# Modulation of layer 0 as 32-bit matmuls of unsplit weights on four column tiles of the array

## The reference, cut to what matters

```python
def ada_params(cond, w, b):
    mod = jax.nn.silu(cond) @ w + b          # w: 2048 x 6144
    return jnp.split(mod, 3, axis=-1)        # shift, scale, gate

sh_l, sc_l, g_l = ada_params(c, ada_w[0], ada_b[0])
sh_c, sc_c, g_c = ada_params(c_ctx, ada_w[0], ada_b[0])
xm_l = x_lat * (1.0 + sc_l) + sh_l
xm_c = x_ctx * (1.0 + sc_c) + sh_c
...
mem_n = rmsnorm(mem, norm_mem_w)             # mem: 256 x 2048
k = mem_n @ w_k                              # 2048 x 2048
```

## Time and profile before

| | us |
|---|---|
| median of 3 runs | 3157.62 |
| the runs | 3156.45, 3160.35, 3157.62 |
| span of the profiled execution | 3157.5 |
| PE busy, share of the span | 98% |
| DVE busy, ACT busy | 70%, 52% |
| first "w" unit starts on PE | 24.88 |
| last "a" unit ends on PE, "w" unit 22 starts | 165.45 |

### The profile page before, as it was taken

How to read it: one execution, slowest core, us unless ns; L and a number is a source line. 1 busy time by engine, 2 the same in 40 slices (tenths; PEclk the granted TensorE clock), 3 DMA queues, 4 the chain that set the end, 5 groups by cost and what they waited for, 6 DMA issues and landing times.

```text
span 3157.5 us, 45097 instructions
## 1 busy us (share of the span) xinstructions
PE 3086.2 (98%) x16842; PEld 2654.5 (84%) x16842; DVE 2218.5 (70%) x2768; ACT 1640.1 (52%) x2000; POOL 53.6 (2%) x52
## 2 busy tenths in 40 slices
PE   7999999999999999999999999999999999999998
PEld 6788878888788887888888888888888888888887
DVE  7779877788677777656757855567456777777544
ACT  6665444546534566544556655445345555555443
POOL 0011300000000000000000000000000000000000
PEclk9999999999999999999999999999999999999999
DMA  8978675787568765655555565566345555555554
GB/s 297 351 249 287 239 276 201 282 323 237 176 221 282 254 203 181 206 173 189 172 188 172 168 199 187 189 226 197 135 150 184 187 186 186 187 191 194 189 190 139
DMA packets 180248, 666.42 MB, mean 211 GB/s; under 512 B 20084, under 2 KB 20468, under 8 KB 178808
## 3 DMA queue, kind: packets, MB, share of 16 engines
q1 hardware_dynamic: 178424, 660.09, 61.7%
q10 hardware_dynamic: 1664, 4.19, 0.3%
HBM read 657.91 MB, written 6.29 MB: 210 GB/s over the span
## 4 chain that ended last, share of the span: by engine, by line
PE 85%; DVE 7%; DMA 4%; ACT 2%; DVEq 1%; issue 1%; ACTq 0%; SPq 0%
PE acc L762 45%; PE acc L766 22%; PE acc L773 4%; PE acc L775 4%; PE acc L774 4%; DVE w_lo L1990 3%; DMA ada_raw<-in_w_ada 2%; ACT w_hi L1277 1%; DMA mod_raw<-in_w_mod 1%; DVE mod_raw L2001 1%; PE acc L930 1%; DMA raw<-in_w_mix_out 0%; PE msc L1172 0%; PE msc L876 0%; PE msc L1192 0%
## 5 line engine op out<-in xcount | busy, mean ns | idle before, releaser
L1990 DVE TENSOR_TENSOR w_lo<-raw,w_hi 128x1024 fp32r<-128x1024 f32 x1020 | 1242.3, 1227 | 564.1 <-ACT w_hi L1277 554.6
L1277 ACT CAST w_hi<-raw 128x1024 fp32r<-128x1024 f32 x1020 | 1061.8, 1049 | 805.6 <-PE acc L766 571.3
L762 PE MATMUL acc<-a_pair,w_hi 128*128 128x512 f32 x2944 | 931.6, 398 | 4.6 <-DVE a_pair L2905 2.4
L766 PEld LDWEIGHTS acc<-a_pair,w_lo 128*128 128x128 f32 x2944 | 554.1, 188 | 131.1
L766 PE MATMUL acc<-a_pair,w_lo 128*128 128x256 f32 x2944 | 579.3, 278 | 0.0
L762 PE MATMUL acc<-b_pair,w_hi 128*128 128x512 f32 x1792 | 569.4, 399 | 5.3 <-DVE w_lo L1990 5.2
L762 PEld LDWEIGHTS acc<-a_pair,w_hi 128*128 128x128 f32 x2944 | 451.2, 189 | 7.6 <-DVE a_pair L2905 2.8
L762 PE MATMUL acc<-f_pair,w_hi 128*128 128x512 f32 x1408 | 442.4, 395 | 0.0
L766 PEld LDWEIGHTS acc<-b_pair,w_lo 128*128 128x128 f32 x1792 | 337.5, 188 | 79.8
L766 PE MATMUL acc<-b_pair,w_lo 128*128 128x256 f32 x1792 | 353.0, 278 | 0.0
L766 PEld LDWEIGHTS acc<-f_pair,w_lo 128*128 128x128 f32 x1408 | 264.5, 188 | 62.5
(11 more groups left out here) (364 smaller groups left out, 2749.5 us busy)
## 6 DMA issues: line engine op xcount, KB each, us to landing
raw<-in_w_ffn_up SPq DMA_DIRECT2D x176, 512.0 KB, 3.9
mod_raw<-in_w_mod SPq DMA_DIRECT2D x128, 512.0 KB, 5.2
raw<-in_w_ffn_down SPq DMA_DIRECT2D x88, 512.0 KB, 3.3
ada_raw<-in_w_ada SPq DMA_DIRECT2D x64, 512.0 KB, 5.5
raw<-in_w_xa_k SPq DMA_DIRECT2D x32, 512.0 KB, 6.1
raw<-in_w_k SPq DMA_DIRECT2D x32, 512.0 KB, 4.6
raw<-in_w_v SPq DMA_DIRECT2D x32, 512.0 KB, 4.8
raw<-in_w_even_out SPq DMA_DIRECT2D x32, 512.0 KB, 4.6
```

The costliest lines, as they stand in the source:

```text
L762: pe.matmul(acc[:, bank(stage, g) + m, :], w_h[:, cols], pair[:, :, kc, :], start=begin, stop=False, skip_group_check=True)
L766: mm = pe.matmul(acc[:, bank(stage, g) + m, 0:T], w_l[:, cols], pair[:, 0, kc, :], start=False, stop=end, skip_group_check=True)
L1277: nc.scalar.copy(w_hi[:, slot], source).then_inc(hi_done, 1)
L1990: vec.tensor_tensor(w_lo[:, slot], source, w_hi[:, slot].bitcast(F32), ALU.subtract).then_inc(lo_done, 1)
```

## The change

The "a" units leave the walk of `mem_k`, which has 32 places now instead of 96. They keep the four buffers `ada_raw`, but these are now a ring of their own: PE reads them directly as 32-bit operands, without rounding and subtraction by ACT and DVE, and frees them itself (`ada_used`). Two units (a pair, four chunks of 128 rows) are taken by four matmuls of 32 stationary columns each (`cond_tile`, two of them filled), one for each quarter of the output partitions: the four chunks' partial sums land on partitions 0 to 31, 32 to 63, 64 to 95 and 96 to 127 of the same PSUM bank. Four pairs make a group of 512 columns. ACT copies all 128 partitions of a group to `mod_rows`; PE multiplies each 128 x 128 block of it with `mod_pick`, a matrix of zeros and ones with two columns, which turns the rows into columns and adds the four partial rows.

```diff
-ADA_FIRST = 6
+ADA_TILES = 4
...
-    Stage("mem_k", "w_xa_k", "F", 1, groups=4, ada=(0, ADA_UNITS), dve=1),
+    Stage("mem_k", "w_xa_k", "F", 1, groups=4, dve=1),
...
+ADA_PAIRS = ADA_UNITS // 2
+ADA_AT = {j: range(j * ADA_PAIRS // ADA_OVER, (j + 1) * ADA_PAIRS // ADA_OVER) for j in range(ADA_OVER)}
+GROUP_PAIRS = DC // ADA_TILES
+ADA_LAST = {g: next(j for j in ADA_AT if GROUP_PAIRS * (g + 1) - 1 in ADA_AT[j]) for g in range(ADA_GROUPS)}
...
-CTX_LOAD_AT = 84
-MEM_SQUARE_AT = {2: 0, 5: 1, 8: 2, 11: 3}
-MEM_SUM_AT = {7: 0, 10: 1, 13: 2, 15: 3}
-MEM_ROOT_AT, MEM_SCALE_AT, MEM_TURN_AT, MEM_TAKE_AT = 16, 17, 22, 27
+CTX_LOAD_AT = 21
+MEM_SUM_AT = 2
+MEM_ROOT_AT, MEM_SCALE_AT, MEM_TURN_AT, MEM_TAKE_AT = 3, 3, 6, 8
+
+MOD_ROWS_AT = {}
+for _g, _j in ADA_LAST.items():
+    MOD_ROWS_AT.setdefault(max(_j, 1), []).append(_g)
+MOD_SUM_AT = {}
+for _j, _gs in MOD_ROWS_AT.items():
+    MOD_SUM_AT.setdefault(min(max(_j + 2, MEM_TAKE_AT + 1), CTX_AT - 2), []).extend(_gs)
...
             def load_first(stage):
 
+                load_mem()
                 for j, (kind, g, k, _) in enumerate(stage.kinds):
...
+                    if j >= RING:
+
+                        sp.wait_ge(lo_done, j + 1)
+                    nc.sync.dma_start(raw[:, j % RING].rearrange("p a b -> p (a b)"),
+                                      t[stage.weights][stage.group_units * g + k]).then_inc(raw_landed[j % RING], 16)
+                    if j == 0:
+                        load_constants()
+                    for pair in ADA_AT.get(j, ()):
+                        for n in (2 * pair, 2 * pair + 1):
+                            if n >= ADA_RING:
+
+                                sp.wait_ge(ada_used, (n - ADA_RING) // 2 + 1)
+                            nc.sync.dma_start(ada_raw[:, n % ADA_RING].rearrange("p a b -> p (a b)"),
+                                              t["w_ada"][n]).then_inc(ada_landed[n % ADA_RING], 16)
...
+            def modulation(pair):
+
+                g, quarter = divmod(pair, GROUP_PAIRS)
+                if quarter == 0:
+
+                    pe.wait_ge(ada_free, g + 1)
+                if pair == 0:
+                    pe.wait_ge(act_step, AFTER["cond"]["act"])
+                for n in (2 * pair, 2 * pair + 1):
+                    pe.wait_ge(ada_landed[n % ADA_RING], 16 * (n // ADA_RING + 1))
+                for tile in range(ADA_TILES):
+                    n, c = 2 * pair + tile // KU, tile % KU
+                    rows = slice(tile * (P // ADA_TILES), (tile + 1) * (P // ADA_TILES))
+                    mm = pe.matmul(msc[rows, 1 + g % 3, :], cond_tile[:, ADA_TILES * quarter + tile, :],
+                                   ada_raw[:, n % ADA_RING, c, :], start=(quarter == 0), stop=(quarter == GROUP_PAIRS - 1))
+                mm.then_inc(ada_used, 1)
+
             def mem_sums(j):
...
+                for pair in ADA_AT.get(j, ()):
+                    modulation(pair)
+                if j == MEM_SUM_AT:
+                    pe.wait_ge(consts_in, 48)
+                    for q in range(4):
...
+                for g in MOD_SUM_AT.get(j, ()):
+
+                    pe.wait_ge(ada_free, 3 + g + 1)
+                    if g == 0:
+
+                        pe.wait_ge(dve_step, AFTER["mem_norm"]["dve"])
+                    for c in range(4 * g, 4 * g + 4):
+                        mm = pe.matmul(msc[:, 0, T + 2 * c:T + 2 * c + 2], mod_rows[:, c * P:(c + 1) * P], mod_pick,
+                                       start=True, stop=True)
...
+                for g in MOD_ROWS_AT.get(j, ()):
+
+                    act.wait_ge(ada_used, GROUP_PAIRS * (g + 1))
+                    nc.scalar.copy(mod_rows[:, g * NCOL:(g + 1) * NCOL], msc[:, 1 + g % 3, :]).then_inc(ada_free, 1)
```

More of the change, by code:

```diff
@@ L99, in __init__ @@
             groups, group_units = 2 * groups, group_units // 2
-        self.group_units, self.groups, self.ada, self.gate = group_units, groups, ada, gate
+        self.group_units, self.groups, self.gate = group_units, groups, gate
         self.n_w = groups * group_units
         self.kinds = [("w", *divmod(n, group_units), (n + 1) % group_units == 0) for n in range(self.n_w)]
[L104 to L112, removed]
         if gate:
@@ L189, in ring_place @@
 def ring_place(stage, j):
[L191 removed]
+    return stage.u0 + j
 def spread(n, k):
@@ L219 @@
 STATES_AT = 9
-assert all(kind[0] == "w" for kind in STAGE["mem_k"].kinds[MOD_TURN - 1:])
+assert max(MOD_ROWS_AT) < MOD_TURN
 KV_GROUP = {"mem_k": 0, "mem_va": 4, "mem_vb": 5}
@@ L469, in build @@
         mod_raw = sb("mod_raw", [P, MOD_RING, KU * NCOL])
-        mod_rows = place("mod_rows", [4, 32 * P], F32, cond_wide_at)
+        mod_rows = place("mod_rows", [P, 32 * P], F32, cond_wide_at)
         assert at[0] - cond_wide_at >= 32 * P * 4
@@ L710, in run @@
                             side(j)
-                        if kind == "a":
-                            ada_bank = 1 + g % 3
-                            if first:
-                                pe.wait_ge(ada_free, g + 1)
-                            pe.wait_ge(lo_done, i * stage.n + (u + 1 + RING))
-                            for c in range(KU):
-                                kc = KU * k + c
-                                pe.matmul(msc[:, ada_bank, :], cond_pair[:, kc, :], w_hi[:, slot, c, :],
-                                          start=(first and c == 0), stop=False)
-                                mm = pe.matmul(msc[:, ada_bank, :], cond_pair[:, kc, :], w_lo[:, slot, c, :],
-                                               start=False, stop=(last and c == KU - 1))
-                            mm.then_inc(unit_used, 1)
-                            continue
                         if kind == "x":
@@ L823, in mem_sums @@
                     steps.end("mem_norm")
[L824 to L829 removed]
+                for g in MOD_SUM_AT.get(j, ()):
[5 more added lines that the diff above has]
+                                       start=True, stop=True)
+                    if g == ADA_GROUPS - 1:
+                        steps.done(mm)
+                        steps.end("mod")
             run("mem_k", b_pair, 0, batch=2, side=mem_sums)
```

133 lines of the change are left out of this document (47 added, 86 removed).

## The result

The changed kernel takes 3182.26 us, the median of four runs (3176.46 to 3187.03), against 3158.98 for the kernel before in the same session (3156.45 to 3161.31): ratio 1.0074, 95% interval 1.0063 to 1.0086. It is slower by 23 us. Four runs more in another session gave 1.0073 (1.0052 to 1.0094). The profiled execution of the changed kernel is the slowest of its four, with a span of 3185.2 us, 27.7 above the span before.

The account below looks back on a forecast made before the run. PE, with DMA and DVE near their limits: start and work 160.5, waits 9, 3.6 and 4.4, clock 5.5 put "w" unit 22 at 183.0 against 165.45; less 1.3 back, 3157.5 + 16.3 = 3173.8 us, range 3155 to 3216.

Parts of the forecast that it names:

- the start of "w" unit 22: First stage, PE, after the last modulation units: any shift moves the program's end equally; forecast 183.0 us against 165.45 before.
- the alternation: PE switching tiling mode between "w" units and pairs, 44 times: 0.3 us a place taken, 6.6 us up to unit 22.
- The step on the pairs: Four 32-bit matmuls per pair on PE: only neighbouring tiles' records overlap, 2.15 us alone, 1.72 where another follows, 64.5 in all.
- the first rival: Pairs on PE: four column tiles run wholly in parallel, 0.86 us a pair, transfers set the time; 3160 us, chance 0.26.
- the half overlap: Pairs on PE: a tile's second record overlaps the next tile's first, 2.15 us a pair alone; the forecast, 3166 to 3184, chance 0.42.
- The rival of tiles wholly beside each other: Pairs on PE at 0.86 us each; transfers bound the stage, two-pair ring runs dry; 3160 us, range 3154 to 3168, chance 0.26.
- the wait at place 9: First 0/1 matmuls: PE idle about 9 us for DVE's scale copy, behind unit 11's subtraction, its transfer queued behind pair 15.
- The other waits: PE waiting for ACT's copies to `mod_rows` at places 12 to 21, 3.6 us, and for the context, 4.4 us.
- The clock term: PE's lower clock after idleness at the start, place 9 and the context: three times 1.6 to 2.1, 5.5 us.
- Tiles one after the other: Pairs on PE: the four column tiles don't overlap, 3.45 us a pair; 3214 us, chance 0.20.
- The queue stays fed: Transfers of the first stage: tiles wholly parallel and dry times mostly covered; 3143 us, floor 3135, chance 0.12.
- After unit 22: PE's 32 transposes (2.11 us) become one group of eight records (0.86): 1.3 us back, and no slack to absorb the delay.

## Why the prediction was right, and where it was not

Forecast were 3173.8 us, range 3155 to 3216, with 0.68 for slower. The time was 3182.3, slower by 0.74%. Sign and range hold, and the size is off by 8.5 us. The moment that the prediction summed, the start of "w" unit 22, was forecast at 183.0 and came at 191.4. That looks like a small miss of one term, and is the sum of large misses with opposite signs:

| term, us | forecast | in the trace |
|---|---|---|
| first pair starts | 15 | 15.1 |
| 22 "w" units and the alternation | 61.2 + 6.6 | 66.0 (22 x 3.0) |
| pairs | 64.5 | 32 (32 x 1.0) |
| squares, transposes of the scale | 7.2 | 7.2 |
| seven groups of 0/1 matmuls | 6.0 | 6.4 (0.92 each) |
| PE's waits | 17.0 | 39.8 |
| lower clock | 5.5 | 24.9 |
| "w" unit 22 | 183.0 | 191.4 |

The middle rows give the work at the higher clock; the last term is what units (15.6), groups (4.8) and pairs (4.5) took beyond it.

- **The step on the pairs failed.** It said that a tile's two records follow each other and records start in order, so that tiles half overlap and a pair costs 2.15 us alone. It costs 1.00. The Trainium skill ("TensorEngine Tiling (Array Packing)", Key Properties) says that different tiles can load and multiply in parallel. The trace agrees, with 1.00 us against 3.55 us on one tile. I had its result as the first rival, and should have given it the larger chance; the half overlap rested on a guess about the order of starts that no row showed.
- **The rival of tiles wholly beside each other had the right mechanism and the wrong price.** It said: PE is no longer the bound, the transfers are, and the queue runs dry because two pairs fit the ring. It counted 25 us of dry time and 3160. The last two pairs landed near 181.6, against its 138.5 us for a queue that never stops: 43 us dry. It counted the squares, place 9 and the later waits once each, at full clock. It left out the lower clock behind the waits: eight units took 4.1 to 5.4 us instead of 3.0, and the next pair was freed that much later. And it left out how often the ring runs short, since SP can ask for a pair only when PE has finished the one two before it: PE waited for pairs 14 times after the first one.
- **The forecast's closeness is therefore luck**: 34 us too much for pairs, "w" units and alternation against 42 us too little for waits and clock. The forecast had PE's own matmuls as what makes the stage long, and they are not; the direction came out because the wait at place 9 and the clock had been seen, at too low a price.
- **The wait at place 9 was right**, place, releaser and size: about 9 us forecast, 9.85 measured, behind the subtraction of unit 11, whose transfer stood in SP's queue behind pair 15. What I made of it was too little: I priced the wait itself and one spell of lower clock. It also stops the refill of a ring of two pairs; taking it away brought unit 22 forward by 14 us, and a third pair, which leaves the wait at 9.65 us, by 31.
- **The other waits**: 4.70 us for the context against 4.4; ACT's copies 7.7 against 3.6.
- **The clock term was mis-sized**, three spells and 5.5 us forecast. It fell at the three places named, and also at places where PE had only waited 2 to 3 us (the 71.35 row has 3.14 us of idleness ahead of it) or 1.68 us for ACT's copy at 109.85.
- **Tiles one after the other**: 3214 forecast, 3217.8 measured with one tile. **The queue stays fed**: its floor was given as 3135, with unit 22 at 144.5; the version with three pairs and spread groups gives 3135.8 and 141.8, with a queue that moved 381 GB/s from 60 to 150 us where 370 had been taken. That case was real, but not for the changed kernel.
- **After unit 22** 1.3 us were to come back, and 1.5 did (25.9 to 24.4). Nothing took up the delay, as forecast.

## What to carry to other kernels

When work leaves the engines that used to release a buffer, look at who releases it now: a ring whose consumer also waits for other things needs more entries than one whose consumer does not, and its depth is to be sized together with the change, not kept. How deep is deep enough no run here shows; four pairs were not tried. Before weighing the engine's own work, ask what the queue does while the engine waits. Here one pair more in the ring was worth 30 us, of which a ring of that depth gave the kernel before 5 too, while 33.5 us more of matmuls cost some 6, within the spread. A deeper ring does not make the waits free: taking PE's waits away was worth another 14 us. Steps that collect results (here the 0/1 matmuls) belong neither right behind their producer nor, by the traces, all at the end, but a few places later.

## What the runs showed of the hardware that I had not expected

- **Column tiles overlap almost fully with 32-bit operands too.** Four matmuls of two records each, 512 columns, take 1.00 us on four tiles and 3.55 us on one. Changing between the full array and four column tiles costs little: a "w" unit between pairs takes 2.99 us against 2.78 before, where all matmuls use the full array, 0.2 us a place.
- **The clock can be at its lower level after short idle times.** In the changed kernel PE was idle 2.09 us ahead of 57.47 and 3.14 us ahead of 71.35, and unit matmuls behind both took 1.05 us instead of 0.63; behind the 9.85 us at place 9 unit 9 took 5.04 us. In the version with spread groups, idle times of up to 1.67 us between 50 and 130 us left the next pair at 1.06 or 1.07 us.
- **It also falls without any idleness, behind a row of 0/1 matmuls.** In that version 24 of their records stand at 80.48, with no wait on PE since 71.53, and unit 12 behind them runs at the lower level: its first matmuls take 1.09 us (the row at 83.18) and the unit 4.53 instead of 2.98. The 64 in a row at 144.17, in the version with three pairs and all groups at place 23, ran mostly at the lower level too. Part of the lower clock at the groups of the changed kernel may be of this kind, and not of waiting; no run separates the two.
- **A matmul that moves two columns is no cheaper than one that moves 128.** A group of eight records with 128 x 128 stationary took 0.92 us at the higher clock, 0.115 us a record, and about 1.73 at the lower; a record that moves 128 columns takes 0.107. That the load of the stationary side sets this is likely, but no run varies it. 64 in a row, partly at the lower clock, are 9.5 to 11.5 us, four to five times what 32 transposes of four rows took the earlier trace rows.
